# Recurrence tiles between the k steps of the input projection

## The reference, cut to what matters

```
proj = rms_norm(x) @ w_in_ab                 # 1024 -> 2560: q, f, i, g, p, 512 each
log_f = logaddexp(log lb, log1p(-lb) + log_sigmoid(f));  k = (1-lb) * sigmoid(-f);  q = silu(q) * 128**-0.5
# per head (4 heads, state 128 x 128), per token:
S_t = diag(f_t) S_{t-1} + k_t v_t^T;  o_t = S_t^T q_t        # samples start from state_hgrn
o = rms_norm_per_head(o, out_gain) * silu(g)
y = (trailing means of p over 2, 4, 8, 16 tokens - p) @ pool_w * pool_scale   # 4 groups of 128
x = x + concat(o, y) @ w_out_ab
```

## Time and profile before

| | us |
|---|---|
| median of 3 runs (range) | 3157.08 (3157.02 to 3157.95) |
| the profiled execution | 3157.28 |
| its span | 3155.5 |
| busy in the span: PE, DVE, POOL, ACT | 2962.7, 1589.6, 849.2, 695.1 |

### The profile page before, as it was taken

One profiled execution on the slowest core, in us unless ns is written; L12 is line 12 of the kernel. 1 busy time (PEld: TensorE's weight loads), 2 busy tenths in 40 slices (PEclk: granted clock), 3 DMA queues, 4 the chain that ended last, 5 costly groups with the idle time before them and its releaser, 6 DMA issues. The chain is left out here.

```text
span 3155.5 us, 46929 instructions
## 1 busy us (share of the span) xinstructions
PE 2962.7 (94%) x16643; PEld 2893.0 (92%) x16643; DVE 1589.6 (50%) x2823; ACT 695.1 (22%) x1046; POOL 849.2 (27%) x651
## 2 busy tenths in 40 slices
PE   5999778599999999999999999999999999999997
PEld 4999777299999999999999988999999999999997
DVE  5224875644444444444654576555644444444454
ACT  3132332422111111111321121112411111111113
POOL 5212442342222222222321123000422222222223
PEclk8999666699999999999999999999999999999998
DMA  2111001111111111111112111111111111111111
GB/s 87 44 40 37 0 0 37 34 41 43 44 40 41 42 40 40 40 40 44 40 52 70 37 34 34 43 40 43 44 37 44 40 40 43 40 40 43 40 41 69
DMA packets 207285, 129.96 MB, mean 41 GB/s; under 512 B 8851, under 2 KB 204136, under 8 KB 206951
## 3 DMA queue, kind: packets, MB, share of 16 engines
q1 hardware_dynamic: 207207, 128.92, 13.6%
HBM read 120.08 MB, written 8.81 MB: 41 GB/s over the span
## 5 line engine op out<-in xcount | busy, mean ns | idle before, releaser
L596 PE MATMUL bank<-xh,wh 128*128 128x384 f32 x3360 | 774.2, 337 | 34.2 <-DVE wl L981 32.7
L596 PE MATMUL bank<-xl,wh 128*128 128x384 f32 x3360 | 764.7, 335 | 0.0
L596 PE MATMUL bank<-xh,wl 128*128 128x384 f32 x3360 | 764.2, 335 | 0.0
L2004 POOL TENSOR_TENSOR raw<-raw,vec 128x512 f32<-128x512 f32 x280 | 294.8, 1063 | 1465.4 <-DMA raw<-in_w_in_ffn 901.0
L1591 ACT ACTIVATE wh<-raw 128x512 fp32r<-128x512 f32 x416 | 262.1, 630 | 1791.9 <-PE bank L596 1203.1
L596 PEld LDWEIGHTS bank<-xh,wh 128*128 128x128 f32 x3360 | 596.4, 188 | 50.7 <-issue 46.8
L596 PEld LDWEIGHTS bank<-xl,wh 128*128 128x128 f32 x3360 | 600.6, 188 | 0.0
L596 PEld LDWEIGHTS bank<-xh,wl 128*128 128x128 f32 x3360 | 600.1, 188 | 0.0
L981 DVE TENSOR_TENSOR wl<-raw,wh 128x512 fp32r<-128x512 f32 x416 | 318.1, 765 | 523.6 <-ACT wh L1591 523.6
L994 DVE TENSOR_TENSOR xs<-bank,xs 128x384 f32<-128x384 f32 (+1 forms) x672 | 333.0, 551 | 311.0 <-PE bank L621 257.0
L621 PE MATMUL bank<-yh,wh 128*128 128x384 f32 x1152 | 267.2, 340 | 6.7 <-DVE xs L994 2.7
(11 more groups left out here) (226 smaller groups left out, 2802.4 us busy)
## 6 DMA issues: line engine op xcount, KB each, us to landing
raw<-in_w_in_ffn SPq DMA_DIRECT2D x176, 256.0 KB, 2.9
raw<-in_w_out_ffn SPq DMA_DIRECT2D x88, 256.0 KB, 2.7
raw<-in_w_uv_c SPq DMA_DIRECT2D x64, 256.0 KB, 2.8
raw<-in_w_in_ab SPq DMA_DIRECT2D x40, 256.0 KB, 2.9
raw<-in_w_out_c SPq DMA_DIRECT2D x32, 256.0 KB, 2.7
xtok<-in_x_prompt SPq DMA_DIRECT2D x8, 512.0 KB, 6.6
raw<-in_w_out_ab SPq DMA_DIRECT2D x16, 256.0 KB, 2.7
out_y_prompt<-otok SPq DMA_DIRECT2D x8, 512.0 KB, 2.6
```

The lines of the kernel that those rows point to most:

```text
L596: mm = pe.matmul(ps[(sg + tb) % BANKS][:, 0:TB], w[:, place, k * P:(k + 1) * P], r[:, kk, tbs(tb)], start=kk == 0 and c == 0, stop=kk == K ...
L2004: pool.tensor_tensor(r, r, g, ALU.mult).then_inc(w_scaled, 1)
```

## The change

The nine units whose results the first tiles don't need run beside the tiles. Eleven units come first, in the order f, q, and three of i; the last of i, the four of p and the four of g follow, one per tile, with the tile's steps issued between k steps. The samples' tile is the first. Units beside tiles use banks 0 to 3 in turn; bank 4 serves the transposes, outputs, pooled products and head sums one after another, bank 5 the diagonals and state updates, banks 6 and 7 the levels. Exponents of level m+2 are started at level m, across the borders of tiles. The two subtracts of a level become one, with two exps (one of the negative); the state's decay and addition become one operation per head; the samples' score product is one per head. Pooling sums (without padded copies of the prompt) go on POOL in tiles 2 to 5, pooled products on PE in tiles 3, 4, 5 and 7, head norms of the first two token blocks in tiles 6 and 8. The output projection starts with the halves over pooled rows of two units, in which the last head sums lie. All of it is unrolled in place of `Fori`. Cut to its core:

```diff
+        UNITS = (4, 5, 6, 7, 0, 1, 2, 3, 8, 9, 10, 11, 19, 18, 17, 16, 12, 13, 14, 15)
+        TILES = (NT - 1,) + tuple(range(NT - 1))
+        BESIDE = 11
 # sync
+            for j in range(3):
+                unit_pieces(j)
+            sp.wait_ge(acc_free, 24)
             for h in range(HEADS):
                 sp.dma_start(sin_[:, h, 0:SEQ]..., A["state_hgrn"][0, :, h]...).then_inc(sin_loaded, 16)
+            for j in range(3, 15):
+                unit_pieces(j)
...
 # tensor
+            def beside(j, after):
+                for h in range(2):
+                    pe.wait_ge(w_high_ready, 2 * j + h + 1)
+                    pe.wait_ge(w_low_ready, 2 * j + h + 1)
+                    for k in range(4):
...
+                        after(kk)
+            def outputs(p):
+                pe.wait_ge(level_in, FIRST[p + 1])
+                pe.wait_ge(eqd_ready, p + 1)
+                pe.wait_ge(kdt_ready, p + 1)
+                pe.wait_ge(v_ready, p + 1)
...
+            def after_first(kk):
...
+                if 3 <= kk <= 6:
+                    sample_update(2 * (kk - 3))
+                    sample_update(2 * (kk - 3) + 1)
...
+            def after_prompt(p, kk):
+                if kk == 0:
+                    pe.wait_ge(o_out, p)
+                    turn_values(p)
+                    pe.wait_ge(state_ready, p)
+                    diagonal(p)
+                if kk < 7:
+                    level(FIRST[p] + kk)
+                if 1 <= kk <= 4:
+                    spare(p, kk - 1)
...
+                if kk == 7:
+                    outputs(p)
+                    state_update(p)
+            for p in range(2, NT):
+                beside(BESIDE + p, lambda kk: after_prompt(p, kk))
...
+            abo_half(0, n0, 1, last_sums(0))
+            abo_half(1, n0 + 1, 1, last_sums(2))
+            abo_half(0, n0 + 2, 0)
+            abo_half(1, n0 + 3, 0)
 # vector, in each tile p, for each level q (m counts levels over all tiles)
+                    scale_queries(m)
+                    if m + 2 < len(LEVELS):
+                        diff(m + 2)
+                    if q == 1:
+                        if p:
+                            take(m - 1)
+                            evict(j - 1)
+                        low(2 * j + 1, 2 * j + 1)
+                    if q == 2:
...
+                            next_state(p - 1)
+                        take_diagonal(p)
+                    if q >= 2:
+                        take(m - 1)
...
 # scalar, in tiles 6 and 8, between the exps of the levels
+                if p in (6, 8):
+                    head_log(p // 2 - 3, x, 4)
...
 # scalar, behind the last tile
+            pool_high(2)
+            for h in range(3):
+                gate_silu(h)
+            outputs(NT - 1)
+            high(n0 + 1, n0 + 1, t0)
+            head_square(2)
+            gate_silu(3)
...
 # vector, behind the last tile
+            take(len(LEVELS) - 1)
+            evict(BESIDE + 8)
+            low(n0 + 1, n0 + 1)
+            pool_low(2)
+            next_state(NT - 1)
+            head_norm(1)
+            low(n0 + 2, n0 + 2)
+            head_norm(2)
+            head_gate(0)
+            head_gate(1)
+            head_low(0)
...
 # gpsimd, in tiles 2 to 5
+                    if 2 <= p <= 5 and q in (3, 4, 6, 7):
+                        k = (3, 4, 6, 7).index(q)
+                        if k <= POOL_ORDER[p - 2]:
+                            window(p - 2, k)
```

More of the change, by code:

```diff
@@ L736, in tile, with diagonal @@
-                if some(t):
-                    pe.wait_ge(o_out, t)
-                if not prompt:
+                    mm = pe.transpose(ps[4][:, h * P:(h + 1) * P], ekd[:, h, :], ident[:, :])
+                mm.then_inc(kd_mm, 1)
+            def diagonal(p):
+                for h in range(HEADS):
+                    mm = pe.matmul(ps[5][:, h * P:(h + 1) * P], work[:, 4 + h, cols(p)], work[:, h, cols(p)],
+                                   start=True, stop=True)
+                mm.then_inc(diag_mm, 1)
@@ L823, in _, with head_sum @@
-            unit(mh, ml, n0 + 2, g0 + 3, n0 + 2, g0 + 3)
-            with pe.Fori(1, 4) as i:
-                abo(i)
+                if tb:
+                    pe.wait_ge(yb_ready, NTB * n + tb)
+                pe.matmul(ps[4][:, 0:TB], poolw[:, gi, :], work[:, 16 + gi, tbs(tb)], start=True, stop=True)\
+                    .then_inc(pool_mm, 1)
+            def head_sum(tb, h, bank):
+                pe.wait_ge(osq_ready, tb + 1)
+                pe.matmul(ps[bank][:, 0:TB], ones[:, :], work[:, 4 + h, tbs(tb)], start=True, stop=True)\
+                    .then_inc(onorm_mm, 1)
@@ L1043, in decay @@
                                            ALU.mult, ALU.add).then_inc(decay_ready, 1)
-            def ab(i, gates=None):
+            for j in range(BESIDE):
+                if j > 1:
+                    low(2 * j + 1, 2 * j + 1)
+                if j:
+                    low(2 * j + 2, 2 * j + 2)
+                for tb in range(NTB):
+                    scaled(work[:, UNITS[j], tbs(tb)], g0 + 3 * j + tb, tb, t0 + 4 * j + 2 + tb)
+                if j in (6, 7):
+                    logf(j - 6)
+                if j in (8, 9):
+                    decay(j - 8)
@@ new lines, in evict, with diff @@
+            def evict(j):
+                for tb in range(NTB):
+                    scaled(work[:, UNITS[j], tbs(tb)], beside_bank(j, tb), tb, t0 + 4 * j + 2 + tb)
+            def diff(m):
+                p, b = LEVELS[m]
+                if m >= 2:
+                    dve.wait_ge(k_scaled, m - 1)
+                    dve.wait_ge(q_scaled, m - 1)
+                bv, ev = blocks(work[:, 20:24, cols(p)], 2 * b), blocks(ediff[:, m % 2], 2 * b)
+                mid = bv[:, :, :, b - 1:b].to_broadcast([P, HEADS, P // (2 * b), 2 * b])
+                dve.tensor_tensor(ev, bv, mid, ALU.subtract).then_inc(diff_ready, 1)
@@ L1047, in ab, with abo @@
+            n0, g0, t0 = PLAN.at["abo"]
+            def abo(i):
+                first = isinstance(i, int)
                 for u in range(2):
-                    first = isinstance(i, int) and i == 0
                     if not first:
                         low(n0 + 4 * i + 2 * u + 1, n0 + 2 * u + 1)
-                    if not first or u == 1:
+                    if not first or u:
                         low(n0 + 4 * i + 2 * u + 2, n0 + 2 * u + 2)
-                    for tb in range(NTB):
-                        scaled(work[:, 2 * i + u, tbs(tb)], g0 + 3 * u + tb, tb, t0 + 8 * i + 4 * u + 2 + tb)
```

1185 lines of the change are left out of this document (656 added, 529 removed).

## The result

The changed kernel takes 3052.49 us (median of 4 runs, 3050.15 to 3054.35) against 3157.05 (4 runs, 3149.82 to 3157.95): ratio 0.9673, 95% interval 0.9657 to 0.969. It is faster by 104.6 us, inside the range, but 31 us short of the forecast of 3021 and outside that case's own 2995 to 3042. The profiled execution took 3050.15 with a span of 3048.4 at a mean granted clock of 0.98.

The account below looks back on a forecast made before the run. Bound: 313 us of recurrence, pooling and head norms bare between dense stages. PE work 259.1, waits 24, less 2.6, then tail 39.3 and 2 for gates, end at 518 instead of 653.7: 3157.1 - 135.7 = 3021, range 2980 to 3074.

Parts of the forecast that it names:

- that case: PE paces the nine tiles, with waits at the hand-overs: 2995 to 3042 us, chance 0.45.
- The main step: Nine of twenty input units run beside the nine tiles, one k step, then one level; whole gain 135.7 us.
- The clock rivals: In the stretch, a quarter of work at half clock, 3076, chance 0.14; or clock low throughout, 3243, chance 0.04.
- PE's own sum: PE work of the stretch: 243.3 us at full clock plus 15.8 for changeovers, 259.1; mid-tile 2.75 per k step.
- hand-over 12, second tile 4, table loads 8: PE's waits: 1.5 x 8 between tiles, 4 for sample state updates, 4 each in seventh and ninth tile for ACT.
- the middle follows PE: Mid-tile, DVE, POOL and ACT need less than PE's 2.75 us per k step, so PE sets the pace.
- Its sign: From the third tile on: a unit evicted every 26 to 30 us, PE over 90% busy, clock above 0.95.
- Events of tiles long past: nothing: Later loads and stores, queued ahead of weight pieces, wait only for events of tiles long past; cost nothing.
- 4 + 2: Before the first output unit's pooled half: 4 us waiting for ACT and DVE, 2 for the last tile's gate activations.
- the rest of the program is unchanged: Only the time from 195.9 us to the second output unit's eviction counts; nothing is taken behind it.
- A fraction of one unit: First eleven units: moved silu, exp and log steps on ACT could make them late by this at most; none taken.
- VectorE paces the tiles: DVE, with contention, needs 27 to 31 us per tile; 4 us more on eight tiles, 3053, chance 0.23.

Follow-up runs that it names:

- e5_copy_before_silu: Changed kernel with ACT's three gate SiLUs moved behind the last tile's output copy, a weight piece's rounding and the head norm's square; 3045.99 us.

## Why the prediction was right, and short

**The main step held.** Nine units fit beside nine tiles and keep most of the clock: 0.84 in the second tile, 0.91 to 1.00 in the others. 457.8 us of stretch became 353.2 by the third unit's evictions, 322.1 forecast. The clock rivals' totals (3076, 3243) are out, and bunching the levels shows how near they were; but their mechanism has a share (below).

**Inside the tiles two errors hid each other.** Counted to the last state update the tiles took 288.0 us, 280.4 forecast, 7.6 over. That small miss is luck in part. The sum had 256.5 us of PE work and 24 of waits. Measured are 34.5 of waits and 253.5 of busy time; busy time weighed with each window's clock gives an estimate of 240 at full clock, and 13 for what the lower clock cost. So PE's work was priced 16 too high, waits 10.5 and the clock 13 too low.

**PE's own sum was high.** A level and a k step take 2.45 us at full clock (level products start at 437.61 and 440.06 in the eighth tile), where the sum had 0.97 + 1.56 + 0.22 = 2.75; over 60 levels that is 18. The terms give 25.9 for a tile before its spare products (12.48 + 6.79 + 1.94 + 0.94 + 1.94 + 1.76) and 27.8 with the eighth tile's three, and that tile took 25.9 in all. The 10 us for the samples' small products were about right, 10.7.

**The clock was put at nothing.** In the second tile it falls from 1.00 (the 5 us from 218.7) with PE busy throughout, in the products of 16 columns:

```profile
228.70:233.70 5.00, 5.00 (x25) 5.00 (x25) 0.00 (x0) 0.00 (x0) 0.00 (x0) 0.50 0.00 0
233.70:238.70 5.00, 5.00 (x20) 5.00 (x21) 0.00 (x0) 0.60 (x1) 0.00 (x0) 0.50 0.17 52
```

The unit's k step behind them ran at the lower clock too. The prediction had these products "at half though PE is busy throughout", priced them between the two levels of the clock, and left what follows them at the higher.

**The waits were placed wrongly.** Taken: hand-over 12, second tile 4, table loads 8. The second tile's waits for DVE's state updates are 4.0, the loads were 7.3 by the run without the logarithm. At the hand-over PE waits 7.4 in all, 3.8 of it between the third and fourth tile and nothing behind the seventh. The step that failed is "the middle follows PE": the prediction named POOL's ten window adds beside DVE, priced them only as a bound, and left out that a pooled product waits for ACT's copy of the one before. The adds cost 16.7 us, nearer 19 with what that run's clears put back. Its sign, PE over 90% busy from the third tile on at a clock above 0.95, came in the sixth and eighth tile alone.

**"Events of tiles long past: nothing" was wrong in kind.** The stores of the samples' states hold POOL for 9.6 us in the third tile. By the trace little of that reaches PE, 0.83 us; no run shows it by itself.

**The tail was mis-sized by clock and contention.** Two gaps came out as forecast, 6.3 us before the pooled halves (4 + 2) and 4.7 before the o half (5). But behind the first the clock fell: 20 products in 6 us where 31 fit, 2.1 us lost. And a gate and a low part took 3.80 each beside POOL's sums where 1.36 and "1.4 to 2.3" were taken, 5.1 us by the run with late sums. The trace of before had the price: the 2.27 of the earlier trace rows is a mean over eight low parts that took 1.35 alone and up to 3.82 beside POOL's sums. That is 7.2 of the 8.9.

**The third output unit was left out.** The working stopped at the second ("the rest of the program is unchanged"). The rest was unchanged, but before, POOL's last sum ended at 643.97, 2.7 us behind the first unit's eviction at 641.24, and the second unit kept PE busy for 12.5 us more; ACT's third square waited for POOL there too (6.2 us), unseen by PE. Now half of the second unit is done ahead, PE has 6.4 us left behind the first eviction (531.54), and the last sum ends 13 us behind it: 9.6 us. The step that failed is where the stretch was cut.

**The start** came 3.8 us late: PE waits 1.94 and 0.58 us for weight low parts in the tenth and eleventh unit. "A fraction of one unit", yes.

**The rival whose number came out.** "VectorE paces the tiles" said 3053. Its cause is half there: contention with POOL, on four tiles and in the tail. But DVE has slack (10.5 us for 32 more), 18.9 of the missing 31 (16.4 by the tail's traces) came back by orders of ACT and POOL in the tail, and tiles without window sums run at PE's 26. A total that agrees is no sign for a mechanism.

For the table, the Trainium skill (ScalarE: Activation LUTs, "Table sets: the hidden batching unit") lets a log and an exp share a load. The trace disagrees here too. In this window of the seventh to ninth tile the log's line reloads for seven of its eight logarithms, and the exps behind them as often, 14 loads in all:

```profile
L1884 ACT ACT_TABLE_LOAD x7 | 9.0, 1283 | 0.1
...
L1856 ACT ACT_TABLE_LOAD x2 | 2.6, 1283 | 0.0
L1860 ACT ACT_TABLE_LOAD x2 | 2.6, 1283 | 0.0
```

## What to carry to other kernels

Dense work laid between the steps of a latency-bound chain pays twice, in cover and in clock, and it must be laid finely: five steps in a bunch gave back 39 of 105 us. A pace read from starts is worth checking in the sum: 0.3 us too much per k step, 60 times, hid waits that weren't foreseen. Before summing, ask of each slow elementwise stream on POOL which DVE operation now stands beside it. And follow the sum past the stretch that is changed, until both kernels keep the same distance: work that was free under the old wait (here POOL's sums, ACT's SiLUs) is next on the path, and an order of instructions, no less work, gets it back.

## What the runs showed of the hardware

One idle stretch of PE of 6.3 us was followed by 6 us at clock 0.56; in the same place, after 2.9 us idle, it stayed at 1.00. The length of the wait alone doesn't tell: behind the same 1.77 us in the o half three products took 0.77 us in the changed kernel and 1.30 in `e5_copy_before_silu`. Nor does being busy: in the second tile the clock was 0.50 over 10 us with PE 100% busy. In the bunched tiles it was 0.73 in the third and 0.80 to 0.85 in the others, in the interleaved ones with the same products up to 1.00, so a wait of PE can cost more than its length (3.4 us less of it brought the first output unit 4.8 sooner). VectorE's operation of 1152 columns took 1.35 us alone and 3.80 beside POOL's sums, a 512-column subtract 0.69 and 2.85; POOL's own sums took 2.6 to 3.7 us. A switch between log and exp cost 1.28 us each way.
